# The second block's context in-projection inside the expert loop, two interleaved threads behind it, and lists of 48 places

## The reference

```
h = rmsnorm(stream) * gain + shift
f_in, f_gate, g_u, g_v, g_gate, c_q, c_kv, k_rope, a_gate = split(h @ w_in[l])      # 1024 x 2208
f = (fourier(f_in) @ w_fmix) * silu(f_gate)
g = spatial_gate(g_u, layernorm(g_v)) * silu(g_gate)
q, k, v = from rmsnorm(c_q) @ w_uq, rmsnorm(c_kv) @ w_ukv, normed by head, rotated for x
x = x + gate * (concat(f, g, attend(q_x, [k_y, k_x], [v_y, v_x]) * silu(a_gate)) @ w_out[l])
y = y + gate_c * (... attend(q_y, k_y, v_y) ...)                                   # layer 0 only
```

## Time and profile before

| | us |
|---|---|
| median of 3 runs (2076.14 to 2079.84) | 2076.82 |
| the profiled execution | 2080.19 |
| its span, first to last instruction | 2078.0 |
| TensorE's busy time, mean granted clock | 1746.3, 0.919 |
| layer 0's experts, about | 300 to 790 |
| layer 1's experts | 1055 to 1540.5 |
| second block | 1540.5 to 2078 |

### The profile page before, as it was taken

The page is one execution under the profiler, slowest core; times in us unless marked ns, Lnnn a source line. Parts: engine busy times, 40 slices in busy tenths (PEclk is TensorE's granted clock), DMA queues, the critical chain, the costliest instruction groups (busy, mean ns, idle before and its releaser), DMA issues.

```text
span 2078.0 us, 17774 instructions
## 1 busy us (share of the span) xinstructions
PE 1746.3 (84%) x7322; PEld 838.6 (40%) x7322; DVE 443.6 (21%) x881; ACT 356.4 (17%) x769; POOL 92.7 (4%) x165
## 2 busy tenths in 40 slices
PE   3996779898898884998899888888856988997888
PEld 1742343333333323745443333333313545544554
DVE  1006430000000003013320000000013227613272
ACT  1003111001001001024110100000012024502341
POOL 1011010000000001122000000000010000010000
PEclk7998879999999997999889999999988998999989
DMA  9987159999999998887259999999975310033200
GB/s 355 353 320 292 57 219 423 420 425 422 421 424 422 421 384 292 309 318 238 98 229 424 423 421 424 424 420 425 423 274 214 115 53 1 1 133 128 94 1 21
DMA packets 115955, 584.92 MB, mean 281 GB/s; under 512 B 9732, under 2 KB 12876, under 8 KB 91288
## 3 DMA queue, kind: packets, MB, share of 16 engines
q1 hardware_dynamic: 88056, 478.01, 56.6%
q0 software_dynamic: 17568, 88.88, 11.8%
q10 hardware_dynamic: 10240, 16.79, 2.2%
HBM read 565.72 MB, written 17.92 MB: 281 GB/s over the span
## 4 chain that ended last, share of the span: by engine, by line
PE 51%; DMA 34%; DVE 8%; ACT 3%; issue 2%; POOL 1%; SPq 1%; ACTq 0%; DVEq 0%; POOLq 0%
PE psum L1546 49%; DMA ring<-in_expert_w_gate 15%; DMA ring<-in_expert_w_up 14%; ACT work L1123 2%; DMA work<-in_ada_w 1%; DMA ring<-in_ada_w 1%; DVE small L725 1%; DVE work L1284 1%; DVE work L1285 1%; DMA work<-mod_scratch 1%; PE psum L861 0%; DMA mod_scratch<-rows 0%; DMA work<-in_w_mod 0%; DMA expert_rows<-work 0%; PE psum L887 0%
## 5 line engine op out<-in xcount | busy, mean ns | idle before, releaser
L1546 PE MATMUL psum<-ring,work 128*64 128x512 f32 (+4 forms) x4160 | 1159.2, 606 | 110.9 <-DMA ring<-in_expert_w_up 77.3
L1546 PEld LDWEIGHTS psum<-ring,work 128*64 128x64 f32 (+2 forms) x4160 | 440.4, 157 | 759.2 <-issue 738.5
L1546 PE MATMUL psum<-work 128*128 128x256 f32 (+6 forms) x1136 | 228.0, 364 | 8.1 <-ACT work L1123 3.4
L1123 ACT ACTIVATE work<-psum 128x512 f32<-128x512 f32 (+5 forms) x296 | 149.9, 518 | 340.8 <-PE psum L1546 145.3
L1546 PEld LDWEIGHTS psum<-work 128*128 128x128 f32 (+2 forms) x1136 | 156.1, 189 | 104.2 <-issue 69.3
L1546 PE MATMUL psum<-work,ring 128*128 128x256 f32 (+1 forms) x640 | 159.0, 408 | 1.8 <-ACT work L1123 1.8
L1208 ACT ACTIVATE work<-psum 128x256 f32<-128x256 f32 x64 | 24.5, 383 | 792.0 <-PE psum L1546 792.0
L1446 DVE TENSOR_TENSOR work<-work,psum 128x256 f32<-128x256 f32 x64 | 26.9, 421 | 596.6 <-ACT work L1208 596.6
L1546 PEld LDWEIGHTS psum<-work,ring 128*128 128x128 f32 x640 | 122.7, 194 | 43.7 <-issue 26.1
L1454 DVE TENSOR_TENSOR work<-psum,rows 128x512 f32<-128x512 f32 x64 | 44.3, 692 | 309.9 <-PE psum L1546 309.9
L1546 PE MATMUL psum<-work,small 128*1 128x512 f32 (+1 forms) x512 | 71.6, 648 | 18.6 <-DMA work<-in_ada_w 10.2
(11 more groups left out here) (232 smaller groups left out, 775.7 us busy)
## 6 DMA issues: line engine op xcount, KB each, us to landing
ring<-in_expert_w_gate SPq DMA_DIRECT2D x64, 2048.0 KB, 18.4
ring<-in_expert_w_up SPq DMA_DIRECT2D x64, 2048.0 KB, 21.6
ring<-in_expert_w_down SPq DMA_DIRECT2D x64, 2048.0 KB, 22.6
work<-in_ada_w POOLq DMA_DIRECT2D x40, 1024.0 KB, 8.7
work<-in_w_mod POOLq DMA_DIRECT2D x16, 1024.0 KB, 5.1
expert_rows<-work ACTq DMA_DIRECT2D x128, 128.0 KB, 6.2
ring<-in_w_in SPq DMA_DIRECT2D x8, 2048.0 KB, 8.2
ring<-in_diff_w_in SPq DMA_DIRECT2D x6, 2048.0 KB, 31.5
```

The costliest lines, as they stand in the source:

```text
L1123: copy = lambda o_, i_: nc.scalar.activation(o_, i_, ACT.Copy)
L1546: return T.matmul(out_, lhsT, rhs, start=start, stop=stop, skip_group_check=True)
```

## The change

- **Lists of 48 places** (LIST). `hS`, `sel`, the gathers and the stores into `expert_rows` are cut from 64 to 48 places an expert; gate, up and down still work on 64 columns, 16 of them zeros or the neighbour's. The padding of `hS` is zeroed ahead of each router (`V.memset`). The overflow branch now begins at a list above 48 (NOVER is 4 steps an expert, 3 before).
- **The context stream's in-projection in layer 1's experts.** POOL loads the context and its norm rows once the last norm of layer 1 is done. ACT squares it before the router's exps; DVE norms one tile in expert 0 and one in expert 1; PE turns it before experts 3 and 4 and does two fills of a section before experts 6, 11, 16, 21 and 26 (Y0_AT), in banks 4 and 7. Each section is one more load in the ring, freed by ACT after its evictions. `expert_item` counts the ring's items with them. DVE's squares of c and v fall into expert 29.
- **Threads.** A pass p is one stream of one layer: 0 is y and 1 is x in layer 0, 2 is y and 3 is x in layer 1. A fill is cut in two halves of 4 chunks. The tables X0_IN, Y0_OUT and X1_IN say how many steps of the other thread follow each half; steps 0 to 14 (FRONT) are the heads, the rest attention. So: x's fills of layer 0 with y's heads and attention; y's out-projection with x's heads; x's attention alone, with y's norm of layer 1 and its two kv fills in it; x's out-projection with y's units; x's fills of layer 1 with its heads; its attention; its out-projection.
- **Storage.** Weights of the second block go through 2 ring slots instead of 3 (WEIGHTS2: the load of item r waits for the use of item r - 2); fills rotate through 2 banks instead of 4, attention's product with v through 1 instead of 2, units' tokens through 2 buffers instead of 3.
- **Norm tiles** of the second block are written by chunk (`by_chunk`, a strided view), one tile at a time, as in the first block (L1284, L1285), and x is normed first. x is stored in four parts of 256 KB.

The diff is cut to its core; helpers that the pieces call (`take_fill`, `c_squares`, `c_norm`, `v_squares`, `v_norm`, `fill_mm`, `turn_c`, `unit_mm`, `unit_turn`) hold the same operations as before for one stream.

```diff
+LIST = 48
+NOVER = -(-(S - LIST) // SLOTS)
...
+    ORDER = (("kv", "gq", "gv", "f", "a"), ("gq", "gv", "f", "a", "kv"), ("kv",), ("kv", "gq", "f", "gv", "a"))
+    Y0_AT = (6, 11, 16, 21, 26)
+    Y0_BANKS = (4, 7)
...
+    FILLS = [("in", 1)] * 10 + [("out", 0)] * 4 + [("in", 2)] * 2 + [("out", 1)] * 4 + [("in", 3)] * 10 + [("out", 3)] * 4
...
+    WEIGHTS2 = ([(1, s_) for s_ in ORDER[1]] + [(0, 0), (0, 1), (2, "kv"), (1, 0), (1, 1)] + [(3, s_) for s_ in ORDER[3]]
+                + [(3, 0), (3, 1)])
...
+    FRONT = 15
+    X0_IN = share_steps([0, 1, 1, 1, 1, 1, 2, 2, 2, 2, 2, 3, 3, 3, 3, 3, 1, 1, 1, 1])
+    Y0_OUT = share_steps([0, 0, 2, 2, 2, 3, 3, 3])
+    X1_IN = share_steps([0] * 11 + [1, 1, 1, 1, 2, 2, 2, 1, 4])
...
+        for r, (p, what) in enumerate(WEIGHTS2):
+            if r >= 2:
+                sp.wait_ge(*weights_used(r - 2))
...
+        for n in range(2 * TT):
+            i, hf = n // 2, n % 2
+            sp.wait_ge(sem("out_used"), nth("out_used", 3, n + 1))
+            sp.dma_start(out[0, i * P:(i + 1) * P, hf * 512:(hf + 1) * 512], x[:, i, hf * 512:(hf + 1) * 512]).then_inc(sem("out"), 16)
...
+    def stream_scale(dve, link, p, t):
+
+        by_chunk = lambda r: r.rearrange("p (c k) -> p k c", k=KT)
+        k = p % 2 * TT + t
+        dve.wait_ge(sem("rms2"), nth("rms2", p, t + 1))
+        link(nc.vector.reciprocal(rs2[:, k:k + 1], rs2[:, k:k + 1]))
+        link(nc.vector.scalar_tensor_tensor(h2[p % 2][:, t, :].rearrange("p (k c) -> p k c", k=KT), by_chunk(stream(p)[:, t, :]),
+                                            rs2[:, k:k + 1], by_chunk(rows[:, 0, :]), ALU.mult, ALU.mult))
+
+    def stream_shift(p, t):
+
+        h_ = h2[p % 2][:, t, :].rearrange("p (k c) -> p k c", k=KT)
+        nc.vector.tensor_tensor(h_, h_, rows[:, 1, :].rearrange("p (c k) -> p k c", k=KT), ALU.add).then_inc(sem("h2"), 1)
...
+    def turn_stream(pe, p, ts, banks):
+
+        for i in range(TT):
+            pe.wait_ge(sem("h2"), nth("h2", p, i + 1))
+            for t in ts:
+                ins = nc.tensor.transpose(bank[banks[(t - ts[0]) // 2]][:, (t % 2 * TT + i) * P:(t % 2 * TT + i + 1) * P],
+                                          h2[p % 2][:, i, t * P:(t + 1) * P], ident)
+                if i and t % 2:
+                    ins.then_inc(sem("h2T_mm"), 1)
...
+        for t in range(TT):
+            stream_rms(act, link, 1, t)
+        take_turned(act, copy, 1, range(KT), (2, 3, 4, 5))
+        for n, js in enumerate(X0_IN):
+            if n % 2:
+                take_fill(act, link, copy, 1, n // 2, n // 2 % 2)
+            for j in js:
+                front(0, j) if j < FRONT else attention(0, j - FRONT)
+        c_root(act, link, 1)
+        v_root(act, 1)
+        for n, js in enumerate(Y0_OUT):
+            for j in js:
+                front(1, j)
+        for t in range(TT):
+            stream_rms(act, link, 2, t)
+        for k in range(19):
+            attention(1, k)
+            if k in (13, 15):
+                take_turned(act, copy, 2, range(2 * k - 26, 2 * k - 22), (0, 1))
+        for n in range(TT):
+            take_fill(act, link, copy, 2, n, (IN_AT[2] + n) % 2)
+        c_root(act, link, 2)
+        stream_rms(act, link, 3, 0)
+        take_c(2)
+        take_unit(2, 0)
+        take_unit(2, 1)
+        stream_rms(act, link, 3, 1)
+        take_turned(act, copy, 3, range(KT), (0, 2, 4, 5))
+        for n, js in enumerate(X1_IN):
+            if n % 2:
+                take_fill(act, link, copy, 3, n // 2, (IN_AT[3] + n // 2) % 2)
+            if n == 1:
+                unit_root(2, 0)
+                unit_root(2, 1)
+            if n in (3, 5):
+                unit_turned(2, n // 2 - 1)
+            if n == 9:
+                c_root(act, link, 3)
+            if n == 17:
+                v_root(act, 3)
+            for j in js:
+                front(3, j)
+        for k in range(18):
+            attention(3, k)
...
+        gain2(dve, link, 1)
+        for t in range(TT):
+            stream_scale(dve, link, 1, t)
+            stream_shift(1, t)
+        c_norm(dve, link, 0)
+        v_norm(dve, link, 0)
+        for n, js in enumerate(X0_IN):
+            for j in js:
+                front(0, j) if j < FRONT else attention(0, j - FRONT)
+        attention(0, 19)
+        c_squares(dve, link, 1)
+        v_squares(dve, link, 1)
+        c_norm(dve, link, 1)
+        v_norm(dve, link, 1)
+        for n, js in enumerate(Y0_OUT):
+            if n % 2:
+                update(0, n // 2)
+            for j in js:
+                front(1, j)
+        for k in range(20):
+            attention(1, k)
+            if k == 2:
+                gain2(dve, link, 2)
+            if k in (4, 8):
+                stream_scale(dve, link, 2, k // 8)
+            if k in (6, 10):
+                stream_shift(2, k // 8)
+        c_squares(dve, link, 2)
+        update(1, 0)
+        c_norm(dve, link, 2)
+        update(1, 1)
+        gain2(dve, link, 3)
+        update(1, 2)
+        stream_scale(dve, link, 3, 0)
+        stream_shift(3, 0)
+        update(1, 3)
+        stream_scale(dve, link, 3, 1)
+        stream_shift(3, 1)
+        unit_squares(2, 0)
+        unit_squares(2, 1)
+        unit_norm(2, 0)
+        unit_norm(2, 1)
+        c_squares(dve, link, 3)
+        c_norm(dve, link, 3)
+        for n, js in enumerate(X1_IN):
+            if n == 16:
+                v_squares(dve, link, 3)
+            if n == 18:
+                v_norm(dve, link, 3)
+            for j in js:
+                front(3, j)
+        for k in range(20):
+            attention(3, k)
+        for n in range(2 * TT):
+            update(3, n)
...
+        def front(p, j):
+
+            if j == 0:
+                turn_c(p)
+            elif j in (1, 2, 5, 8):
+                unit_mm(p, (1, 2, 5, 8).index(j))
+            elif j in (3, 6, 9):
+                fourier(p, j // 3 - 1)
+            elif j in (4, 7, 10, 13):
+                unit_turn(p, (j - 4) // 3)
+            elif j == 11:
+                spatial(p)
+            else:
+                turn_mix(p, (j - 12) // 2)
...
+        pe.wait_ge(sem("proj"), every("proj", 0))
+        turn_stream(pe, 1, range(KT), (2, 3, 4, 5))
+        pe.wait_ge(sem("h2T"), every("h2T", 1))
+        for n, js in enumerate(X0_IN):
+            in_half(1, n)
+            for j in js:
+                front(0, j) if j < FRONT else attention(0, j - FRONT)
+        pe.wait_ge(sem("a_o"), every("a_o", 0))
+        for n, js in enumerate(Y0_OUT):
+            out_half(0, n)
+            for j in js:
+                front(1, j)
+        for k in range(19):
+            attention(1, k)
+            if k in (12, 14):
+                if k == 14:
+                    pe.wait_ge(sem("h2T"), nth("h2T", 2, 2))
+                turn_stream(pe, 2, range(2 * k - 24, 2 * k - 20), (0, 1))
+            if k >= 17:
+                if k == 17:
+                    pe.wait_ge(sem("h2T"), every("h2T", 2))
+                in_half(2, 2 * (k - 17))
+                in_half(2, 2 * (k - 17) + 1)
+        pe.wait_ge(sem("a_o"), every("a_o", 1))
+        for n in range(8):
+            out_half(1, n)
+            if n in (4, 5, 7):
+                turn_c(2) if n == 4 else unit_mm(2, n // 2 - 2)
+        turn_stream(pe, 3, range(KT), (0, 2, 4, 5))
+        pe.wait_ge(sem("h2T"), every("h2T", 3))
+        for n, js in enumerate(X1_IN):
+            in_half(3, n)
+            if n in (3, 5):
+                unit_turn(2, n // 2 - 1)
+            for j in js:
+                front(3, j)
+        for k in range(19):
+            attention(3, k)
+        pe.wait_ge(sem("a_o"), every("a_o", 3))
+        for n in range(8):
+            out_half(3, n)
...
+            if l and e in Y0_AT:
+                k = Y0_AT.index(e)
+                n, s_ = y0_item(k), ORDER[0][k]
+                room(n)
+                sp.dma_start(section(0, s_), w_in_part(0, s_)).then_inc(sem(f"loaded{slot(n)}"), 16)
+            n0 = expert_item(l, e, 0)
...
+                pool.wait_ge(sem("h_done"), TT * 4)
+                pool.dma_start(y_raw, a["ctx_2"][0].rearrange("(t p) d -> p t d", p=P)).then_inc(sem("y_in"), 16)
+                norm_rows(pool, 0)
+                row_load(3, a["final_norm_g"].rearrange("(a n) -> a n", a=1).to_broadcast((P, D)), "norm_in")
                 ada_store(LAST1)
-                pool.wait_ge(sem("h_done"), TT * 4)
-                row_load(3, a["final_norm_g"].rearrange("(a n) -> a n", a=1).to_broadcast((P, D)), "norm_in")
+                pool.wait_ge(sem("v_ss"), 1)
+                norm_rows(pool, 1)
...
+                if l and e in (3, 4):
+                    take_turned(act, copy, 0, range(4 * e - 12, 4 * e - 8), Y0_BANKS)
+                if l and e in Y0_AT:
+                    k = Y0_AT.index(e)
+                    for i in range(TT):
+                        take_fill(act, link, copy, 0, TT * k + i, Y0_BANKS[i])
```

(21 more changed lines are left out.)

1099 lines of the change are left out of this document (561 added, 538 removed).

## The result

The changed kernel took 2007.72 us (median of 4 runs, 2005.66 to 2012.08) beside 2078.01 for the kernel before (2076.14 to 2079.84): a ratio of 0.9665, 95% interval 0.9644 to 0.9685, 70 us less. A second set of five runs, beside other experiments, gave 2009.14 and again 0.9665 (0.965 to 0.968). The forecast was 2007. The total is right; it is a sum of terms of which some missed by 8 to 13 us and cancelled. The profiled execution took 2005.66, with a span of 2003.8.

A forecast was written before the change was run, and what follows sets the result against it. The prediction took DMA bytes to bound the experts and PE to decide afterwards; experts ending at 1547.0, x's first fill at 1582.8 and the thread stages summed to 2008.5, carried over to 2007 us, own range 1995 to 2018.

The forecast's parts named there:

- Part 1, lists: Both expert loops and opening gathers: lists of 48 places save 7.7 us a layer, 5.4 of it from smaller stores.
- Part 2, the sections in the loop: Layer 1's experts: 9.04 MB of added loads cost 21.4 us, PE's fills hide; with shorter lists +14.2 us.
- Up to the loop: Stretch before layer 1's first gate matmul: the forecast's terms up to there make it 9.5 us earlier.
- Part 3, to x's first fill: From the last expert to x's first fill: 35.8 us instead of 36.5, with DVE's strided norm the late thing.
- Part 4, the threads: From x's first fill to the end: stage times in PE's order with interleaved threads, from 112 us to 32.2 us.
- the second half wait 2 us for its weights: Context out-projection: two ring slots instead of three make PE wait 2 us for the second half's load.
- the hand-overs: Between the threads after the experts: some 90 hand-overs of 0.05 us, +4 us (0 to 8).
- Table loads: ScalarE after the experts: 19 table loads instead of 12, taken as hidden; 51 us if all were exposed.
- Threads hide little: Rival for the interleaved threads: head steps wait on ACT and heads cost what they did, 2032 us; chance 20%.
- PE-bound experts: Rival for layer 1's experts: added work costs its 64 us of PE instead of 21.4, 2049 us; chance 7%.
- Everything hides: Rival for the stages after the experts: only PE's own work counts, 33 us less, 1974 us; chance 11%.
- The overflow branch: Rival in either layer: an expert above 48 tokens reloads all experts, 2480 us; 2% together with other losses beyond 70 us.

The follow-up runs named there:

- experiment 1: The changed kernel with its lists put back from 48 to 64 places, all else kept: 2019.21 us, ratio 0.9721.
- experiments 11 and 12: The changed kernel with lists of 40 places instead of 48: 2015.92 us; the same, but each store again writing 48 rows: 2005.34 us.
- experiment 2: The changed kernel with the context stream's ten fills of layer 0 cut to one of eight chunks, all loads kept: 2006.63 us, ratio 0.9659.
- experiment 3: The changed kernel with the five context section loads in layer 1's experts cut to an eighth of their bytes, fills kept: 1992.36 us, ratio 0.9581.
- experiment 6: The changed kernel with x's norm rows loaded later and the second block's first weights requested only after the gather's rows landed: 1996.69 us, ratio 0.9601.
- experiment 8: The changed kernel with the second block's norm tiles in plain order and transposes reading every eighth column: 1999.72 us, ratio 0.9619.
- experiment 7: The changed kernel with x's sections in the first thread ordered gq, f, a, gv, kv instead of gq, gv, f, a, kv: 2005.72 us, ratio 0.9648.
- experiment 4: The changed kernel with its three interleavings taken apart, all fills first, then all head and attention steps: 2048.26 us, ratio 0.9859.
- experiment 10: The changed kernel with two sections behind the experts, moved transfers, reordered sections, plain norm tiles and an earlier x gain row: 1982.59 us, ratio 0.9538.
- experiment 5: The changed kernel with two of the context stream's five sections moved from layer 1's expert loop to behind the experts: 1996.42 us, ratio 0.9597.

## Why the prediction came out right, and where it was off

**Part 1, lists.** Forecast -15.4 us for both layers, measured 11.6 by the ratio and 9.6 by the traces (experiment 1). That smaller stores and a smaller opening gather give the gain is right in both halves; the loops' part was 7.9 instead of 10.8, and the gathers' 1.7 instead of 5.0, as their clock differed. That it is bytes is not what experiments 11 and 12 show: 40 rows are fewer bytes than 48 and cost more, and rows per DMA engine fit all three.

**Part 2, the sections in the loop.** Mechanism right: loads bind (experiments 2 and 3), fills are free, though PE is close to its own limit (experiment 3). The size was off by 8.7: from first gate matmul to last eviction 510.1 against 501.4. Three pieces are measured. The shorter lists gave 1 us less here than their term. x's norm rows, 1.05 MB that POOL issues at 1518.5, inside the loop, were not in my sum; moving them (experiment 6) took 3.4 us off the loop. And PE waited 5.35 us for the last expert's weights where before it waited 1.14 (at 1526.99), and did its gate and up matmuls at the lower clock, 8.97 us instead of 7.09: 1.9 for the slower matmuls. The rest, 2 to 3 us, is more than layer 1's loop varies between equal kernels (0.4 us): while the loads ran, the DMA engines moved 418 GB/s (1051 to 1542 us) where they had moved 420 before (1063 to 1532), which is 2 to 3 us over 205 MB. Why the rate is lower is open. The forecast's step was "It adds 9.04 MB of loads; at the loop's rate of two experts' 13.10 MB in 31.0 us (422 GB/s) +21.4 us": it counted the sections and not every DMA that moved with them.

**Up to the loop.** Layer 1's first gate matmul came 11.4 us earlier (1055.1 to 1043.7), where the forecast's terms up to there make 9.5. 3.6 of it lie before layer 0's router, where the change does nothing, and the lists gave less; the stretch between the two loops varied from 272 to 277 us between executions of kernels that don't differ in it. So what lies beyond the lists' part of these 11.4 us is variation from execution to execution, not something that was forecast. With the loop's 8.7 the experts ended at 1553.8 instead of 1547.0.

**Part 3, to x's first fill.** 37.6 us against 35.8. The strided norm is on the chain as forecast (and experiment 8 prices it at 1.6 a tile); missed was that SyncE, no longer held back by the row load, asks for a 2 MB load of the second block and ten small ones between 1553.1 and 1565.9 us, in front of and among the gather's four parts (1560.7 to 1564.5), the last of which then takes 8.41 us instead of 5.2. The step that failed is the gather taken over from before at its old duration: its neighbours on the queue had changed. Experiment 6 gives these us back.

**Part 4, the threads.** 412.4 us from x's first fill against 425.7. x's first thread 108.5 (112), context out-projection 52.6 (58), attention 42.8 (45), gap 12.8, last in-projection 90.5 (90.7), the two last stages to 0.5 us. Missing was a term for the clock: x's first thread ran 9.7 us at 1.2 GHz, 4.9 us lost (experiment 6), and still came out shorter than forecast. Too dear were the context out-projection, where I let DVE's 43 us of work decide and let the second half wait 2 us for its weights: PE was busy 50.0 of 52.6, its load had been issued in time at 1698.97; and the hand-overs, for which I had 4 us and none shows. Too cheap was x's out-projection, 35.7 instead of 33.5: the one slot wait that I had foreseen for both is here:

```profile
1800.88 8.00 DMA ring<-in_w_out
```

PE waited 1.2 us at the end of that load; the stage's PE work was 34.5 us where I had 31.7.

**Table loads.** 19 behind x's first fill, as counted, each 1283 ns. (Before, the trace has 14 behind the last eviction, where the prediction counted 12.) They were hidden but for little: experiment 7 took two away, and PE's idle time in that thread fell by 0.8 us; the rest of the 3.5 us was clock. At the 2.66 us a switch that the Trainium skill gives (ScalarE: Activation LUTs, "What ACT_TABLE_LOAD costs") 19 exposed would have been 51 us, an estimate. The trace has the exp 1.30 us behind the start of its table load (1674.28 to 1675.58), so the price here is the 1.28.

**The rivals.** "Threads hide little" (2032) is refuted by experiment 4: they hide 37 us. "PE-bound experts" by experiment 2. "Everything hides" was near in two stages (108.5 and 52.6 us where it had 107 and 52); of the 13.3 us that the tail from x's first fill gained on the forecast, the loop (8.7) and the hand-over (1.8) took most back. That the total came out within 1 us of 2007 is luck: the profiled span is 2003.8 where the sum had 2008.5, and its two largest misses have opposite signs. The overflow branch was not entered.

**Where the 70 us come from.** By ratio: 11.6 from the lists, 40 from the interleaving (37 by the trace), and the remaining 18 from the place of the context in-projection and what went with it (the row load and the context norms in front of x): some 60 us of PE work left the tail, and the loop paid its bytes. That third part is only what the first two leave; no run undid it alone.

## What to carry to other kernels

A loop bound by DMA bytes takes PE work for nothing as long as PE's own sum stays below that of the bytes, but charges for every byte that comes with it: count each transfer that moves into it, small row loads too, and look first whether PE has a wait elsewhere in which both the bytes and the work are free, as behind the last expert here. Before a gain of a few us is put down to an edit, split the stage into PE's idle time and its granted clock: in experiment 7, 2.7 of 3.5 us were clock, and experiment 6 gained as much without that edit. Two chains of dependent small steps are best hidden between long matmul groups of another stream, in halves of 3.5 us; that was worth more (37 to 40 us) than the shorter lists and the moved projection together. When a queue's waits change, recompute the landing time of whatever was quick because that queue was held back.

## What the hardware showed that was not expected

- A store of 40 rows of 2 KB costs about as much as one of 64 and more than one of 48: padding 128 such stores to 48 rows made the kernel 8.5 us faster. Its semaphore is raised 10 times as the data lands (and once at the issue), the others' 16 times.
- TensorE's clock fell to 1.2 GHz while it waited 31.3 us for x and stayed there for the first 6.3 us of x's thread; in experiment 10, with fills in the wait and no gap over 1.5 us behind them, x's whole thread was at 2.4 GHz, 4.6 us shorter. In experiment 5, with gaps of 3.9 and 3.1 us behind such fills, the first 5.1 us of x's thread were again at 1.2 GHz.
- Fewer matmuls made those that stayed slower: without the context fills the granted clock in the loop was 0.94 instead of 0.98.
- Plain against strided reads of 128x1024 f32: 1.28 and 1.22 us against 2.07 and 2.01 on VectorE, no difference for TensorE's transposes (352 and 353 ns).
